# A modulation product, a first normalisation and the input projections put into one block

## The reference, cut to what matters

```
mod = silu(c) @ w_ada + b_ada                 # two rows of 6 * D: c for latent tokens, c_ctx for context
sh1, sc1, g1, sh2, sc2, g2 = split(mod, 6)
h    = rms_norm(x, norm1) * (1 + sc1) + sh1   # (1152, 1024)
proj = h @ w_in + b_in                        # 1024 -> 2960 columns: queries, keys, values, gates, pool input
...                                           # attention, matrix memory, pooling -> w_out -> residual with g1
h2   = rms_norm(x1, norm2) * (1 + sc2) + sh2  # then a router and 16 experts, residual with g2, final norm
```

## Time and profile before

| | us |
|---|---|
| median of 3 runs (1633.96 to 1644.95) | 1642.18 |
| the profiled execution, its own time | 1637.78 |
| its span, first to last instruction | 1635.1 |
| start of the first projection | 132.39 |
| end of the projections' block | 494.3 |
| TensorE busy, share of the span | 86% |
| mean granted TensorE clock | 0.929 |

### The profile page before, as it was taken

One profiled execution on the slowest core, in us unless ns is written; L12 is line 12 of the kernel. 1 busy time (PEld: TensorE's weight loads), 2 busy tenths in 40 slices (PEclk: granted clock), 3 DMA queues, 4 the chain that ended last, 5 costly groups with the idle time before them and its releaser, 6 DMA issues. The chain is left out here.

```text
span 1635.1 us, 18513 instructions
## 1 busy us (share of the span) xinstructions
PE 1402.5 (86%) x7443; PEld 1020.0 (62%) x7443; DVE 620.7 (38%) x1357; ACT 298.4 (18%) x677; POOL 165.3 (10%) x161
## 2 busy tenths in 40 slices
PE   6798999999997999966869997029999999999962
PEld 1124555554576788754844443029999999999931
DVE  0232127011110566656932216503434343334437
ACT  0311000023001344442431102000111011111013
POOL 0005000000000111006300001350000000000030
PEclk9998999999998999967989998559999999999976
DMA  9767611101004312001051003665665776877454
GB/s 324 257 244 245 160 39 39 38 1 39 28 1 92 49 21 40 1 21 55 16 201 43 0 0 120 148 221 177 214 212 196 270 284 235 314 262 297 179 195 166
DMA packets 126598, 222.57 MB, mean 136 GB/s; under 512 B 38789, under 2 KB 56853, under 8 KB 126377
## 3 DMA queue, kind: packets, MB, share of 16 engines
q1 hardware_dynamic: 114047, 182.56, 34.2%
q0 software_dynamic: 11024, 34.03, 5.7%
q10 hardware_dynamic: 1440, 4.78, 0.8%
HBM read 191.32 MB, written 32.96 MB: 137 GB/s over the span
## 5 line engine op out<-in xcount | busy, mean ns | idle before, releaser
L1643 PE MATMUL ps<-sb 128*128 128x128 f32 (+10 forms) x2048 | 284.9, 300 | 1.9 <-ACT sb L1731 1.9
L1643 PEld LDWEIGHTS ps<-sb 128*128 128x128 f32 x2048 | 280.6, 191 | 2.9 <-ACT sb L1731 2.2
L487 PE MATMUL ps<-sb 128*128 128x512 f32 (+1 forms) x576 | 189.2, 491 | 1.9 <-PEq L316 1.9
L490 PE MATMUL ps<-sb 128*128 128x384 f32 (+1 forms) x576 | 173.1, 461 | 0.0
L487 PEld LDWEIGHTS ps<-sb 128*128 128x128 f32 x576 | 95.3, 192 | 96.4 <-issue 95.9
L490 PEld LDWEIGHTS ps<-sb 128*128 128x128 f32 x576 | 108.6, 189 | 63.2
L1650 PE MATMUL ps<-sb 128*128 128x128 f32 (+10 forms) x1024 | 143.5, 300 | 1.2 <-DVE sb L1793 0.9
L1650 PEld LDWEIGHTS ps<-sb 128*128 128x128 f32 x1024 | 139.3, 190 | 2.6 <-DVE sb L1793 2.2
L1231 PE MATMUL ps<-sb 128*128 128x512 f32 x288 | 126.4, 596 | 0.0
L211 PE MATMUL ps<-sb 128*2 128x512 f32 x192 | 89.2, 622 | 24.6 <-DMA sb<-in_w_ada 16.2
L1788 DVE TENSOR_SCALAR sb<-sb 128x128 f32<-128x128 f32 (+10 forms) x64 | 15.7, 245 | 230.3 <-ACT sb L1742 230.3
(11 more groups left out here) (266 smaller groups left out, 1626.6 us busy)
## 6 DMA issues: line engine op xcount, KB each, us to landing
sb<-in_w_down SPq DMA_DIRECT2D x32, 1024.0 KB, 10.8
sb<-in_w_gate SPq DMA_DIRECT2D x15, 2048.0 KB, 11.4
sb<-in_w_up SPq DMA_DIRECT2D x15, 2048.0 KB, 16.4
sb<-in_w_ada SPq DMA_DIRECT2D x12, 2048.0 KB, 8.0
sb<-in_w_in SPq DMA_DIRECT2D x7, 1536.0 KB, 7.9
slot_y<-sb POOLq DMA_DIRECT2D x18, 512.0 KB, 14.1
slot_y<-sb SPq DMA_DIRECT2D x16, 512.0 KB, 5.2
sb<-mod_rows SPq DMA_DIRECT2D x6, 1024.0 KB, 9.5
```

The costliest lines, as they stand in the source:

```text
L487: last = nc.tensor.matmul(bank(i % 8)[0:m, 0:tn], w[:, k, b * m:(b + 1) * m], hT[:, k, t0:t0 + tn], start=(k == 0), stop=(k == KD - 1))
L490: last = nc.tensor.matmul(bank(i % 8)[:, 0:m], hT[:, k, t0:t0 + P], w[:, k, 0:m], start=(k == 0), stop=(k == KD - 1))
L1643: last = nc.tensor.matmul(bank(f % 2)[:, n * CHUNK:n * CHUNK + cols_n], w[:, at:at + P], xT[:, k, 0:cols_n], start=(k == 0), stop=(k == KD ...
```

## The change

The three blocks become one. The edits:

1. x is loaded at once, from SP and ACT in turns, and `w_ada` comes in 24 chunks of 128 x 2048 (one slice of D, a third of the columns), 1 MB each, ring of five. A chunk's product is four products of 512 columns whose outputs are two partitions each at partitions 0, 32, 64 and 96 of one bank ("strips").
2. Group 0 (eight chunks: shift and scale of the first norm) is multiplied before the projections. Groups 1 and 2 are multiplied among the units: one chunk ahead of each of the units 4, 6, ..., 18 and 22, 24, ..., 36, into bank 7; the units take turns in seven banks.
3. The row is not sent through DRAM for the first norm: its strips are turned on TensorE into columns `mcol`, eight slices by two rows. VectorE multiplies x by the inverse root alone; TensorE turns x in chunks of four pieces (one slice of D, 512 tokens; two last chunks for the context); VectorE and ACT in turns take them from PSUM to `hT` with scale and shift, each one number per partition.
4. Unit 0 starts when the first 512 latent tokens are in `hT`; the last six chunks are turned between units 0 and 1.
5. ACT issues the biases and `w_first`. POOL clears `zero_tile` and `qaT` and fills `slot_y` from the block's start; `vb`, `gi`, `gf`, which share memory with the new buffers, are cleared after the last rows of the product are stored, and VectorE waits for that at unit 54.

```
+        RING_BANKS, ADA_BANK = 7, (3, 7, 7)
+        ADA_FIRST = {1: 4, 2: 22}
+        ada_at = {ADA_FIRST[g] + 2 * k: g * KD + k for g in (1, 2) for k in range(KD)}
+        ada_read_at = {ADA_FIRST[g] + 2 * KD - 1: g for g in (1, 2)}
+        def strip(j):
+            return slice(32 * j, 32 * j + 2)
+        def load_ada(sp, i):
+            g, k = divmod(i, KD)
+            if i >= ADA_RING:
+                sp.wait_ge(mod_mm, i - ADA_RING + 1)
+            sp.dma_start(ada[i % ADA_RING], ada_src[:, k, g * GROUP:(g + 1) * GROUP]).then_inc(ada_loaded[i % ADA_RING], 16)
+        def multiply_ada(pe, i):
+            g, k = divmod(i, KD)
+            pe.wait_ge(ada_loaded[i % ADA_RING], 16 * (i // ADA_RING + 1))
+            if k == 0 and g:
+                pe.wait_ge(mod_evac, STRIPS * g)
+            for j in range(STRIPS):
+                last = nc.tensor.matmul(bank(ADA_BANK[g])[strip(j)], cc[:, :, k], ada[i % ADA_RING][:, j * BANK:(j + 1) * BANK],
+                                        start=(k == 0), stop=(k == KD - 1))
+            last.then_inc(mod_mm, 1)
+        def read_ada(dve, g):
+            dve.wait_ge(mod_mm, KD * (g + 1))
+            for j in range(STRIPS):
+                nc.vector.tensor_tensor(mrow[strip(j), g], bank(ADA_BANK[g])[strip(j)], mrow[strip(j), g], ALU.add).then_inc(mod_evac, 1)
...
+        def turn_h(pe, c):
+            if c < 4:
+                pe.wait_ge(x_normed, 4)
+            else:
+                pe.wait_ge(h_by[c % 2], (c - 4) // 2 + 1)
...
+            for n, (t, k) in enumerate(blocks):
+                last = nc.tensor.transpose(bank(h_bank(c))[:, n * P:(n + 1) * P], x_res[:, t, k * P:(k + 1) * P], ident)
+            last.then_inc(x_turned1, 1)
+        def scale_h(engine, c, one):
+            engine.wait_ge(x_turned1, c + 1)
+            if c < 2 * KD:
+                k, t0 = c % KD, 4 * P * (c // KD)
+                ins = one(hT[:, k, t0:t0 + BANK], bank(h_bank(c)), mcol[:, 1, k, 0:1], mcol[:, 0, k, 0:1])
...
+        def front_sp(sp):
+            for v in range(2):
+                sp.dma_start(cc[:, v, :], c_both[v].rearrange("(k p) -> p k", p=P)).then_inc(c_ready, 16)
+            for t in range(0, NT, 2):
+                sp.dma_start(x_res[:, t, :], x_all[t * P:(t + 1) * P, :]).then_inc(x_loaded[0], 16)
+            for i in range(KD):
+                load_ada(sp, i)
+        def front_act(act):
+            act.dma_start(ident, k_ident).then_inc(const_ready, 16)
+            for t in range(1, NT, 2):
+                act.dma_start(x_res[:, t, :], x_all[t * P:(t + 1) * P, :]).then_inc(x_loaded[1], 16)
...                                                  # norm1 as columns, b_ada and norm2 into the strips
+            act.wait_ge(c_ready, 16 * 2)
+            nc.scalar.activation(ce, cc, ACT.Exp, scale=-1.0).then_inc(silu_exp, 1)
...                                                  # the biases of the projections
+            act.dma_start(w_first, ...).then_inc(w_first_in, 16)
...                                                  # squares of x, root
+            for c in range(1, CHUNKS_H, 2):
+                scale_h(act, c, lambda o, i, scale, shift: nc.scalar.activation(o, i, ACT.Identity, bias=shift, scale=scale))
...
+        def front_pe(pe):
+            pe.wait_ge(silu_done, 1)
+            for i in range(KD):
+                if i == KD - 1:
+                    pe.wait_ge(const_ready, 16)
+                    for c in range(4):
+                        turn_h(pe, c)
+                multiply_ada(pe, i)
+            pe.wait_ge(mod_evac, STRIPS)
...                                                  # 16 turns of strip pieces to columns
+            for c in range(4, 12):
+                turn_h(pe, c)
+        def before_unit(pe, i):
+            if i == 0:
+                for way in range(2):
+                    pe.wait_ge(h_by[way], KD // 2)
+            if i == 1:
+                for c in range(12, CHUNKS_H):
+                    turn_h(pe, c)
+                for way in range(2):
+                    pe.wait_ge(h_by[way], KD + 1)
+            if i in ada_at:
+                multiply_ada(pe, ada_at[i])
...                                                  # SP, in the loop over the groups' weights
                     if g == 2:
-                        sp.dma_start(rpb_rows, ...).then_inc(mod_stored, 16)
+                        sp.dma_start(rpb_rows, ...).then_inc(rpb_copied, 16)
+                        for i in range(KD, KD + 10):
+                            load_ada(sp, i)
+                    if g == 3:
+                        for i in range(KD + 10, KD * GROUPS):
+                            load_ada(sp, i)
+                        sp.wait_ge(mod_evac, 2 * STRIPS)
+                        store_mod(sp, 1)
+                    if g == 4:
+                        sp.wait_ge(mod_ready, 2)
+                        store_mod(sp, 2)
...                                                  # POOL
                 nc.gpsimd.memset(zero_tile, 0.0).then_inc(zeros_ready, 1)
                 nc.gpsimd.memset(qaT, 0.0).then_inc(zeros_ready, 1)
-                nc.gpsimd.memset(vb, 1.0).then_inc(zeros_ready, 1)
...
                 pool.wait_ge(slots_zeroed, 16 * (2 + OVER))
+                pool.wait_ge(mod_stored, 16 * 2 * STRIPS)
+                nc.gpsimd.memset(vb, 1.0).then_inc(zeros_ready, 1)
```

More of the change, by code:

```diff
@@ L177, in program @@
         mark_h = ar.at
[L178 to L187, removed]
+        ar.at = mark_h
+        STRIPS, GROUPS, ADA_RING = 4, 3, 5
+        GROUP = STRIPS * BANK
+        c_ready, b_ready = sem("c_ready"), sem("b_ready")
         silu_exp = sem("silu_exp")
         silu_done = sem("silu_done")
-        ada_loaded = [sem(f"ada_loaded{s}") for s in range(2)]
+        ada_loaded = [sem(f"ada_loaded{s}") for s in range(ADA_RING)]
         mod_mm = sem("mod_mm")
@@ L193, in program @@
         mod_ready = sem("mod_ready")
-        mod_stored = sem("mod_stored")
-        x_loaded = sem("x_loaded")
+        mod_stored, rpb_copied = sem("mod_stored"), sem("rpb_copied")
+        x_loaded = [sem("x_loaded_sp"), sem("x_loaded_act")]
         squares, mean_ready, guess_ready = sem("n1_squares"), sem("n1_mean"), sem("n1_guess")
[L198 to L224, removed]
+        x_normed, x_turned1, cols_turned1, cols_ready = sem("x_normed"), sem("x_turned"), sem("mod_cols_turned"), sem("mod_cols_ready")
+        h_by = [sem("h_by_dve"), sem("h_by_act")]
         def newton(st, y, t, ms):
@@ L231, in newton @@
             st.link(nc.vector.scalar_tensor_tensor(out=y, in0=t, scalar=1.5, in1=y, op0=ALU.add, op1=ALU.mult))
[L233 to L289, removed]
@@ L437, in program @@
         bias_row = ar.take([3 * MW + TAIL])
+        early = Arena(sb, after_mlstm_in)
+        early.at = mark_h
+        ada = [early.take([GROUP]) for _ in range(ADA_RING)]
+        mrow, nrow, sq_junk = early.take([GROUPS, BANK]), early.take([BANK]), early.take([D])
+        cc, ce = early.take([2, KD]), early.take([2, KD])
+        ss, y0, nt1 = (early.take([NT]) for _ in range(3))
+        ncol, mcol = early.take([KD]), early.take([2, KD, 2])
+        x_at = after_mlstm_in + HEADS * TOK
+        assert after_proj - x_at == NT * D
@@ new lines, in read_ada, with store_mod @@
+        def read_ada(dve, g):
+            dve.wait_ge(mod_mm, KD * (g + 1))
+            for j in range(STRIPS):
+                nc.vector.tensor_tensor(mrow[strip(j), g], bank(ADA_BANK[g])[strip(j)], mrow[strip(j), g], ALU.add).then_inc(mod_evac, 1)
+        def store_mod(sp, g):
+            for j in range(STRIPS):
+                n = STRIPS * g + j
+                sp.dma_start(mod_rows[:, n * BANK:(n + 1) * BANK], mrow[strip(j), g]).then_inc(mod_stored, 16)
+        CHUNKS_H = 2 * KD + 2
@@ new lines, in scale_h @@
+        def scale_h(engine, c, one):
+            engine.wait_ge(x_turned1, c + 1)
+            if c < 2 * KD:
+                k, t0 = c % KD, 4 * P * (c // KD)
+                ins = one(hT[:, k, t0:t0 + BANK], bank(h_bank(c)), mcol[:, 1, k, 0:1], mcol[:, 0, k, 0:1])
+            else:
+                for n in range(4):
+                    k = 4 * (c - 2 * KD) + n
+                    ins = one(hT[:, k, LAT:TOK], bank(h_bank(c))[:, n * P:(n + 1) * P], mcol[:, 1, k, 1:2], mcol[:, 0, k, 1:2])
+            ins.then_inc(h_by[c % 2], 1)
@@ new lines, in front_dve @@
+        def front_dve(dve):
+            st = dve_steps
+            dve.wait_ge(silu_exp, 1)
+            st.link(nc.vector.tensor_scalar(ce, ce, 1.0, None, ALU.add))
+            st.link(nc.vector.reciprocal(ce, ce))
+            nc.vector.tensor_tensor(cc, cc, ce, ALU.mult).then_inc(silu_done, 1)
+            dve.wait_ge(squares, 1)
+            nc.vector.tensor_scalar(ss, ss, 1.0 / D, EPS, ALU.mult, ALU.add).then_inc(mean_ready, 1)
+            dve.wait_ge(guess_ready, 1)
+            newton(st, y0, nt1, ss)
+            for t in range(NT):
```

(30 more changed lines are left out.)

95 lines of the change are left out of this document (52 added, 43 removed).

## The result

| | before | after |
|---|---|---|
| median, us | 1638.07 (1633.36 to 1644.95, 4 runs) | 1622.49 (1614.08 to 1624.34, 4 runs) |
| ratio, 95% interval | | 0.9885 (0.9861 to 0.9910) |
| profiled execution, and its span | 1637.78, 1635.1 | 1624.34, 1621.9 |
| first projection (unit 0) starts | 132.39 | 93.68 |
| last projection ends | 493.87 | 475.98 |

The change takes 1.15% off (0.90 to 1.39% by the interval), a little more than the one per cent within which the prediction's likeliest class lay. The profiled executions differ by 13.2 us of span: the projections end 17.9 us earlier, and 6.7 us of that are lost again in a stage that the change doesn't touch.

The account below looks back on a forecast made before the run. It took TensorE to bound the projections, after 132.35 us of a relay front. Start -45.3, work between units +4.7 and chunks +29 sum to -11.7 us: 1630 against the median 1642.18, range 1608 to 1665.

Parts of the forecast that it names:

- likeliest class: Whole kernel: the time stays the same within one per cent, 16 us; chance 0.45, against 0.35 faster and 0.20 slower.
- start of unit 0: Front: chunk 7 in at 71 us, then 15.9 us, so unit 0 at 87 against 132.35, 45.3 us earlier.
- work between units 0 and 1: Six more chunks of x turned there: 3.3 us of turns and some 1.4 of context evictions, +4.7 us.
- sixteen chunks among the units: Projections: 1.71 us a chunk plus 0.1 for changing product width, 16 x 1.81 = 29 us, all on the path.
- a transfer issued later, on the other hardware queue, stays behind: Front's loads: w_first goes ahead of chunks 5 to 7, and all the fill before chunk 7, in at 71 us.
- the squares, Newton steps and normalising of x ... run meanwhile and cost nothing: Front: 12 us in ACT and some 8 in VectorE, hidden while the loads up to chunk 7 arrive.
- From the last product on: Front's end: last product, strip reading, turns, column operations and eight chunks of x to unit 0, 15.9 us.
- Strips overlap wholly: Rival: a chunk's four strips take one product's time, 0.86 us, -14.5 us more, 1616 in all; chance 0.17.
- No overlap: Rival: strips run one after another, 27.4 us more in the units and 1.7 in the front, 1659; chance 0.27.
- Everything after the projections is unchanged work: Stages behind the projections, the scan among them: no change in time, 0 us.
- the stall at unit 4: Chunk 8 lands at 106 us, unit 4 comes at about 116; stall rival (or late memsets) 10 to 20 us, 0.06.
- fill hidden: Rival: POOL's fill doesn't hold up the front, chunk 7 at 47 us, strips by halves, 1606; chance 0.10.

Follow-up runs that it names:

- run 2: The changed kernel with POOL's zero fills of slot_y held until group 0's eight products are done: 1590.44 us.
- run 3: The changed kernel with w_first and the seven bias loads issued by SP behind chunk 7 instead of by ACT: 1609.83 us.
- run 4: The changed kernel with norm1 and two bias columns read as contiguous runs, 384 packets instead of 2560 (wrong values): 1610.79 us.
- run 1: The changed kernel with all four products of a chunk written to the first strip (wrong modulation), read to the projections' end only: 519.05 us.
- Run 7: The changed kernel with only an extra wait in the scan, POOL's product behind VectorE's pass of four steps earlier: 1614.08 us, ratio 0.9837 to before.
- run 5: The changed kernel with biases and w_first on SP behind chunk 7, fill held until ten units are done, rpb copy after the last weights: 1580.92 us.
- run 6: run 5's kernel plus the scan's extra wait, POOL's product behind VectorE's pass of four steps earlier: 1572.53 us, ratio 0.9574 to before.

## Why the prediction was right or wrong

The time was 7.5 us below the 1630 predicted and inside the range; 4.1 of these are the median of before, which its fourth run moved from 1642.18 to 1638.07. The likeliest class, within one per cent, was missed by little. The sum came close by luck: three terms failed, and their errors offset each other. The chunks cost 13.5 us less than forecast; the start gained 6.6 us less, and the scan, put at nothing, cost 6.7.

| term | predicted | measured |
|---|---|---|
| start of unit 0 | -45.3 (87) | -38.7 (93.68) |
| work between units 0 and 1 | +4.7 | +4.47 |
| sixteen chunks among the units | +29 | 16 x 0.97 = +15.5 |
| rest, to the end of the projections | 0 | +0.8 |
| **to the end of the projections** | **-11.7** | **-17.9** |
| the scan | 0 | +6.7 |
| other stages | 0 | -2.0 |
| span | -11.7 | -13.2 |

**The start was nearly right for the wrong reasons.** Two steps failed in it, in opposite ways.

The first is "a transfer issued later, on the other hardware queue, stays behind". It rested on the earlier trace rows, 782 packets of ACT's to 38 of SP's from 16 to 25 us. That row counts packets and gives no time of issue; the timeline of before does, for SP's sequencer from 19 to 30 us:

```profile
22.21 7.23 SPq L204 DMA_DIRECT2D sb<-in_w_ada  x2
```

For most of the window SP had little or nothing queued, so the row couldn't show an order. After shows the turn: 975 to 973 to 972. By turns only SP's own packets stand before chunk 7. From the x tiles on they are 5 x 128 of 4 KB and 8 x 128 of 8 KB, 104 an engine, fewer than the fill's 144. So neither ACT's transfers nor all of the fill had to be served first (POOL's queue had moved 6.01 of its 9.44 MB by 51 us), and chunk 7 landed at 50.9, not 71: 20 us to the good. The fill's part in that landing, 24 us in the prediction (71 against 47), is the 12 us of run 2. The same round had been in the prediction for POOL; I used it for two of three queues.

The second is that "the squares, Newton steps and normalising of x ... run meanwhile and cost nothing". Their cover was ACT being free once x is in, at some 20 us. But ACT issues the biases first, and an issue isn't free where many packets stand ahead in its queue: 19.24 us for one. I counted the 4-byte packets as time on the DMA engines (3 us, from the earlier trace rows) and never as turns: alone they go in a moment, next to 8 KB packets each waits for a turn. The squares start at 61.05, chunk 7 is multiplied 29.9 us after it landed. Runs 3 and 4 take that out in two ways and get unit 0 at 64.06 and 67.72, where 87 less the 20 us of the first error is 67.

From the last product on the step held: 93.68 - 80.75 = 12.9 us against 15.9.

**The chunks were mis-sized.** I took two steps out of four to overlap, 1.71 us a chunk and 0.1 for the change of width, 29 us in all; they overlap almost wholly, 0.97 us. "Strips overlap wholly" was a rival at 0.17, with 0.86 us. What I set against it, that the two instructions of one product follow each other in their strip, doesn't hold the other strips up in the rows. The Trainium skill (TensorE: Matmul & The Clock Gate, Part 3: Packing small matmuls) puts the span of matmuls in several strips at one matmul's time and some 4 ns for each further strip; for two instructions of 0.43 us that is an estimate near 0.9 us a chunk. The trace agrees within a tenth, with 0.97. "No overlap", at 0.27, is excluded by run 1: it would have cost 43 us more.

**"Everything after the projections is unchanged work"** was true of the work and not of its time: the scan lost 6.7 us as ten passes instead of one came behind POOL's product. Run 7, which sets the order in the scan and nothing else, takes 8.4 us off.

**Right:** the stall at unit 4 that I weighed (10 us of slack) didn't come at this speed of the front: chunk 8 landed at 105.4 us and was multiplied at 120.7. It came as soon as the front was faster, with 17.17 and 9.81 us in runs 3 and 4. The seven banks and the strips' reading cost TensorE no wait, as costed. The rival "fill hidden" (1606) had its mechanism half right: the fill cost the front 21 us, as run 2 shows, but by turns that held ACT, not by chunk 7's landing. With ACT free it is chunk 7's landing that counts: 50.9 us in run 3, 38.4 in run 5, and unit 0 11.4 us earlier.

## What to carry to other kernels

Before costing an engine's work as hidden, read that engine's own order: the transfers it issues stand in its program like instructions, and one with many packets ahead of it in its queue can hold the engine, for 19.24 us here. Count small transfers in packets against what the other queues hold at that time, not in bytes. And two counts of packets in a window say nothing on order unless both transfers were issued before it began.

## What the runs showed of the hardware

- Three queues with work moved the same number of packets, whatever their size: 975, 973 and 972 packets in 24 us, with 6.46, 3.57 and 0.03 MB.
- Issuing can stop an engine: 19.24 and 16.95 us for one transfer each on ACT, 0.51 and 0.67 where the three columns are 384 packets instead of 2560. What sets the length of an issue, room in the queue for instance, no run separates. On SP in run 3 it took 22.71 us, and chunk 8's issue stood behind it.
- Four column strips with two output partitions each: eight float32 instructions in 0.97 us, one strip 3.54.
- VectorE's pass over two SBUF operands and POOL's product hold each other up. Whichever starts first, with the other engine's work before it done or all but done, runs at its own length (0.56; POOL 0.83), the other ends late (1.21 for either, 1.19 in most of the long passes). In run 6 POOL's product runs beside passes with a PSUM operand and takes 0.83. The Trainium skill (SBUF — State Buffer, SBUF: two separate sides) tells of a port pair that the two hold exclusively for a whole instruction; the rows agree. With the scan's code unchanged, edits of the front alone gave 1, 2, 7 and 10 long passes; what decides it stays open.
- Eight narrow instructions in four strips take 1.04 us where the rows grant the full clock (2.4 GHz) and 1.89 where they grant half: in run 5 at 25.08 us (1.00) and at 27.56 us (0.50, 1.2 GHz; TensorE had been idle from 26.12 on). Over after's first 50 us the rows give 1.00 with 1.89 in each of seven chunks. But the trace of after has no record of the clock before 82.5 us, and a stretch without one prints as 1.00; in before the first record stands at 17.7, where the pitch of the earlier trace rows goes from 0.86 to 0.43 us. So the half clock that the prediction reads there is inferred from the pitch.
